# A hybrid decoder layer on one core: the prologue in the order the first product needs, three weight tiles in three passes each, and two weight pieces exchanged at the border of two products

## What is computed

```python
h = rmsnorm(x, norm_mix_g);  p = h @ w_in           # w_in: 2048 x 5120
o1, o2, o3, o4 = A_WIDTH, 2 * A_WIDTH, 2 * A_WIDTH + B_WIDTH, 2 * A_WIDTH + 2 * B_WIDTH
u = jax.nn.gelu(p[..., :o1]);  v = rmsnorm(jax.nn.gelu(p[..., o1:o2]), sgu_norm_g)
bg, cg, xb = p[..., o2:o3], p[..., o3:o4], p[..., o4:]
y_a = u * chunk_sgu(v, w_s, b_s)
zc, new_mix = causal_dwconv(cg * xb, mix_prev, conv_mix_w, conv_mix_b)
y = concatenate([group_rmsnorm(y_a, ...), group_rmsnorm(bg * zc, ...)], axis=-1)
x = x + y @ w_out
h = rmsnorm(x, norm_ffn_g)
gate, new_ffn = causal_dwconv(h @ w_gate, ffn_prev, conv_ffn_w, conv_ffn_b)
x = x + (jax.nn.silu(gate) * (h @ w_up)) @ w_down   # then a final rmsnorm
```

## Time and profile before

| what | value |
|---|---|
| median of three runs | 2260.38 us (2256.43, 2260.38, 2260.46) |
| the profiled execution | 2259.35 us, of which the span is 2257.7 us |
| PE busy | 2213.3 us, 98% of the span |
| DVE, ACT, POOL busy | 78%, 49%, 24% |
| mean granted clock of TensorE | 0.994 |

### The profile page before, as it was taken

One profiled execution on the slowest core, in us unless ns is written; L12 is line 12 of the kernel. 1 busy time (PEld: TensorE's weight loads), 2 busy tenths in 40 slices (PEclk: granted clock), 3 DMA queues, 4 the chain that ended last, 5 costly groups with the idle time before them and its releaser, 6 DMA issues. The chain is left out here.

```text
span 2257.7 us, 43328 instructions
## 1 busy us (share of the span) xinstructions
PE 2213.3 (98%) x16612; PEld 2199.4 (97%) x16612; DVE 1757.0 (78%) x2354; ACT 1111.4 (49%) x1758; POOL 547.2 (24%) x685
## 2 busy tenths in 40 slices
PE   6999999999999999999999999999999999999997
PEld 6999999999999999999999999999999999999997
DVE  5677777878333998888888888888888798888886
ACT  6454543444211554544445445444544665555565
POOL 4001111212222111111111011111112365555573
PEclk8999999999999999999999999999999999999998
DMA  7444345557433334443535353444446667765433
GB/s 226 100 141 115 113 118 156 181 164 248 133 96 95 115 112 144 138 155 120 159 126 159 118 162 125 149 127 153 137 138 226 205 204 243 233 221 200 165 108 106
DMA packets 377575, 346.05 MB, mean 153 GB/s; under 512 B 10474, under 2 KB 350629, under 8 KB 372720
## 3 DMA queue, kind: packets, MB, share of 16 engines
q1 hardware_dynamic: 346608, 203.98, 31.1%
q0 software_dynamic: 30848, 140.46, 17.4%
HBM read 273.40 MB, written 71.00 MB: 153 GB/s over the span
## 5 line engine op out<-in xcount | busy, mean ns | idle before, releaser
L3017 PE MATMUL ps<-form,dw_hi 128*128 128x288 f32 x1204 | 357.5, 297 | 4.5 <-DVE dw_lo L2458 2.1
L3018 PE MATMUL ps<-form,dw_hi 128*128 128x288 f32 x1204 | 354.4, 294 | 0.0
L3019 PE MATMUL ps<-form,dw_lo 128*128 128x288 f32 x1204 | 353.9, 294 | 0.0
L2956 PE MATMUL ps<-hq,w_hi 128*128 128x288 f32 x1008 | 298.4, 296 | 1.8 <-DVE w_lo L2302 1.8
L2957 PE MATMUL ps<-hq,w_hi 128*128 128x288 f32 x1008 | 296.8, 294 | 0.0
L2958 PE MATMUL ps<-hq,w_lo 128*128 128x288 f32 x1008 | 296.3, 294 | 0.0
L2458 DVE TENSOR_TENSOR dw_lo<-down,dw_hi 128x512 fp32r<-128x512 f32 (+1 forms) x280 | 236.9, 852 | 72.9 <-ACT dw_hi L1101 72.1
L3017 PEld LDWEIGHTS ps<-form,dw_hi 128*128 128x128 f32 x1204 | 225.8, 188 | 6.1 <-issue 5.4
L3018 PEld LDWEIGHTS ps<-form,dw_hi 128*128 128x128 f32 x1204 | 227.6, 189 | 0.0
L3019 PEld LDWEIGHTS ps<-form,dw_lo 128*128 128x128 f32 x1204 | 227.3, 189 | 0.0
L1541 ACT ACTIVATE w_hi<-raw 128x1024 fp32r<-128x1024 f32 x168 | 176.8, 1052 | 74.8 <-DMA raw<-in_w_gate_dram 68.4
(11 more groups left out here) (409 smaller groups left out, 6536.4 us busy)
## 6 DMA issues: line engine op xcount, KB each, us to landing
raw<-in_w_gate_dram SPq DMA_DIRECT2D x88, 512.0 KB, 4.6
down<-in_w_down_dram SPq DMA_DIRECT2D x32, 1024.0 KB, 5.5
form<-act_scratch POOLq DMA_DIRECT2D x28, 1152.0 KB, 7.1
act_scratch<-stage POOLq DMA_DIRECT2D x45, 576.0 KB, 4.7
raw<-in_w_in_dram SPq DMA_DIRECT2D x44, 512.0 KB, 4.8
raw_c<-in_w_up_dram SPq DMA_DIRECT2D x42, 512.0 KB, 3.8
raw_d<-in_w_up_dram SPq DMA_DIRECT2D x42, 512.0 KB, 5.3
raw<-in_w_out_dram SPq DMA_DIRECT2D x30, 512.0 KB, 4.0
```

The lines of the kernel that those rows point to most:

```text
L2956: te.matmul(out, w_hi[:, c, j, :], b_form(t, 0, j), start=start and j == 0, stop=False, skip_group_check=True)
L3017: te.matmul(out, dw_hi[:, m % 4, j, :], act_f[:, j, 0, :], start=start and j == 0, stop=False, skip_group_check=True)
L3018: te.matmul(out, dw_hi[:, m % 4, j, :], act_f[:, j, 1, :], start=False, stop=False, skip_group_check=True)
L3019: last = te.matmul(out, dw_lo[:, m % 4, j, :], act_f[:, j, 0, :], start=False, stop=stop and j == n - 1, skip_group_check=True)
```

## The change

Seven things are different.

1. PE transposes x tiles 0, 1 and 2, then begins. Three weight tiles (0, 1, 2) are worked in the first half and again in the second, each in three passes of 16 matmuls (`pre_part`): high x high over all 16 blocks, then low weight x high h, then high weight x low h. The transposes of x tiles 3 and 4 stand between the second and the third pass of tiles 1 and 2 of the first half. Weight tile 3 follows by `gemm`.
2. Units take banks by a table (X_BANK), so that tile 1 need not wait for tile 0's banks; the pairs of product banks are PRE_PAIR.
3. ACT and DVE take the units by kind of work instead of unit by unit. ACT: three squares, stages 0 to 3, high parts 0 to 7, weight pieces 0 and 1, stage 4, high parts 8 to 11, and on. DVE: all twelve gains, low parts 0 to 7, low parts of weight pieces 0 and 1, low parts 8 to 11, and on.
4. Weight tile 1 (pieces 2 and 3) is loaded into raw_z, which lies over x_nat[1], once x tiles 0 and 1 are transposed; tile 2's high and low parts (w_hi2, w_lo2) lie over x_nat[0] and x_nat[1]. Its reload of `raw` starts as soon as pieces 0 and 1 are split.
5. The column form t4f, which lies in the same place as w_hi2, is now made by ACT after piece 6 is done, and with it DVE's two low forms and all behind them.
6. POOL issues the loads of ws_nat and bias_b ahead of the last four stage transfers instead of behind them.
7. At the border, `raw_y` is loaded with piece 1 and `raw[:,0]` with piece 3; ACT and DVE follow, SP waits one low part longer before its loop, and ACT makes the high parts of the last two blocks of y before the first two weight pieces of the loop instead of behind them.

```diff
-    SKIP = 5 * WVIS + 2
+    SKIP = 5 * WVIS + 4
-        PRE_SLOT = (0, 1, 2, 3, 1, 0, 2, 3)
+        PRE_SLOT = {0: 0, 1: 1, 2: 2, 3: 3, 6: 2, 7: 3}
+        PRE_PAIR = (0, 1, 2, 1)
+        w_hi2 = sb("w_hi2", [P, 2, PK, P], F32R, at=n_at)
+        w_lo2 = sb("w_lo2", [P, 2, PK, P], F32R, at=n_at + 8192)
+        raw_z = sb("raw_z", [P, 2, PK, P], at=n_at + 8192)
+        X_BANK = (4, 5, 6, 7, 0, 1, 2, 3, 4, 5, 6, 7, 1, 3, 6, 7, 5, 6, 7, 5)
...
@@ SP @@
-            for n in range(1, PRE):
-                tile2(w_in, HEADS + n, 2 * n)
+            sp.wait_ge(x_t, 8)
+            for s in range(2):
+                sp.dma_start(raw_z[:, s], col(w_in, HEADS + 1, s)).then_inc(rawz_landed[s], 16)
+            for n in range(2, PRE):
+                for s in range(2):
+                    sp.wait_ge(lo_ready, s + 1 if n == 2 else 2 * n - 1 + s)
+                    sp.dma_start(raw[:, s], col(w_in, HEADS + n, s)).then_inc(raw_landed[s], 16)
...
-            sp.dma_start(raw_y[:, :, :], col(w_out, 1, 1)).then_inc(rawy_landed, 16)
+            sp.dma_start(raw_y[:, :, :], col(w_out, 1, 0)).then_inc(rawy_landed, 16)
             sp.wait_ge(lo_ready, IN_PIECES - 2)
-            sp.dma_start(raw[:, 0], col(w_out, 1, 0)).then_inc(raw_landed[0], 16)
+            sp.dma_start(raw[:, 0], col(w_out, 1, 1)).then_inc(raw_landed[0], 16)
             sp.wait_ge(lo_ready, IN_PIECES)
             sp.dma_start(raw[:, 1], col(w_out, 0, 1)).then_inc(raw_landed[1], 16)
+            sp.wait_ge(lo_ready, IN_PIECES + 4)
...
@@ POOL @@
             for u in range(4 * (TB + 1)):
+                if u == 4 * TB:
+                    pool.wait_ge(x_t, 4 * TB)
+                    g.dma_start(ws_nat[:, :, :], w_s[0].rearrange("h i j -> i h j")).then_inc(late_landed, 16)
...
@@ ACT @@
-            x_square(0)
-            x_square(1)
-            for tb in range(TB + 1):
-                for kq in range(4):
-                    x_unit(4 * tb + kq)
-                    if (tb, kq) in ((0, 1), (2, 3), (3, 1)):
-                        x_square({0: 2, 2: 3, 3: 4}[tb])
...
+            for tb in range(3):
+                x_square(tb)
+            x_stage(range(0, 4))
+            x_hi(range(0, 8))
+            pre_hi(0, 0)
+            pre_hi(1, 0)
+            x_stage(range(4, 5))
+            x_hi(range(8, 12))
+            x_stage(range(5, 8))
+            pre_hi(2, 0)
+            x_square(3)
+            pre_hi(3, 0)
...
+            act.wait_ge(t_sub, 4)
+            act.wait_ge(piece_done, 6)
+            a.activation(t4f[:, 0, :, :], xq(slice(0, PJ), 1, 0), ACT.Copy).then_inc(t_hi, 1)
...
-            first_hi(1, raw[:, 0], (raw_landed[0], 16 * (PRE + WVIS + 1)), (sum_done, 4 * WVIS))
+            first_hi(1, raw_y[:, :, :], (rawy_landed, 16), (sum_done, 4 * WVIS))
...
@@ DVE @@
+            x_gain(range(0, 1))
+            x_diag(1)
+            x_gain(range(1, 6))
+            x_diag(2)
+            x_gain(range(6, 12))
+            for u in range(8):
+                x_lo(u)
+            pre_lo(0)
+            pre_lo(1)
+            for u in range(8, 12):
+                x_lo(u)
+            x_diag(3)
+            pre_lo(2)
+            pre_lo(3)
+            x_gain(range(12, 16))
...
-                    first_lo(1, raw[:, 0])
+                    first_lo(1, raw_y[:, :, :])
...
@@ PE @@
+            def pre_part(tile, half, part):
+                cols = slice(half * HALF, (half + 1) * HALF)
+                for kk in range(KT):
+                    s, k = kk // PK, kk % PK
+                    q = 2 * tile + s
+                    unit = (4 * TB if half else 8) + kk // 4
+                    if part == 0:
+                        if k == 0:
+                            pe.wait_ge(hi_ready, q + 1)
+                        if kk % 4 == 0:
+                            pe.wait_ge(xhi_ready, unit + 1)
+                    elif part == 1:
+                        if k == 0:
+                            pe.wait_ge(lo_ready, q + 1)
+                    elif kk % 4 == 0:
+                        pe.wait_ge(xlo_ready, unit + 1)
...
             for half in range(2):
+                for tile in range(3):
+                    pe.wait_ge(xT_copied, ((5, 7, 9), (13, 14, 20))[half][tile])
+                    pre_part(tile, half, 0)
+                    pre_part(tile, half, 1)
+                    if half == 0 and tile >= 1:
+                        x_transposes(tile + 2)
+                    pre_part(tile, half, 2)
...
+            pe.wait_ge(tile_read, 2)
+            gemm(6, (PRE_SLOT[6], PRE_SLOT[7]), PRE_PAIR[3], mid=corner)
```

More of the change, by code:

```diff
@@ L327, in build_layer @@
         rawx_landed = sem("rawx_landed")
+        rawz_landed = [sem(f"rawz_landed{i}") for i in range(2)]
         rawy_landed = sem("rawy_landed")
@@ L2661, in params_t @@
                 for h in range(HEADS):
-                    last = te.transpose(ps[:, 4 + h // 4, (h % 4) * P:(h % 4 + 1) * P], ws_nat[:, h, :], ident[:, :])
+                    last = te.transpose(ps[:, 6 + h // 4, (h % 4) * P:(h % 4 + 1) * P], ws_nat[:, h, :], ident[:, :])
                 last.then_inc(param_t, 1)
@@ L2691, in _ @@
-            for t in (2, 3):
-                pe.wait_ge(tile_read, t - 1)
-                gemm(2 * t, PRE_SLOT[2 * t:2 * t + 2], t % 2, mid=params_t if t == 2 else corner)
+            def pre_part(tile, half, part):
[14 more added lines that the diff above has]
+                        pe.wait_ge(xlo_ready, unit + 1)
+                    w = pre_lo_of(q) if part == 1 else pre_hi_of(q)
+                    x = h_lo if part == 2 else h_hi
+                    last = te.matmul(pair(PRE_PAIR[tile], half), w[:, k, :], x[:, kk, cols],
+                                     start=part == 0 and kk == 0, stop=part == 2 and kk == KT - 1)
+                    if part == 2 and half == 1 and k == PK - 1:
+                        last.then_inc(piece_done, 1)
```

195 lines of the change are left out of this document (96 added, 99 removed).

## The result

The changed kernel takes 2249.15 us (median of 12 runs, 2243.66 to 2254.81); the kernel before, on the same chip, 2262.66 (12 runs, 2256.43 to 2268.85). The ratio of the runs is 0.9941, 95% interval [0.9928, 0.9953]: faster by 0.6%, 13.3 us. The profiled executions stand 9.96 apart (2259.35 and 2249.39; spans 2257.7 and 2247.8), where the forecast was 11.2. The forecast median of 2249.2 was met by 0.05; how much of that is chance is said further down.

A forecast was written before the change was run, and what follows sets the result against it. PE, busy 98% of the span, bounds the kernel with its waits and slow clock, mostly in the first slice. Prologue 9.9 plus border 1.3 gave 11.2 us: profiled 2259.35 to 2248.2, median 2249.2, range 2244.8 to 2253.0.

The forecast's parts named there:

- The first hole: Prologue, after the 96 transpose rows: PE idles 2.5 us, 20.7 to 23.2, until ACT's high part 8 is done.
- The second hole: Prologue, after the first pass: PE idles 2.1 us, 25.4 to 27.5, until DVE's first weight low part is done.
- the first rival: The clock falls in the new prologue holes; free in the first, 1.5 to 3 us after the second: 2250.7 to 2252.2, chance 0.17.
- No further hole to tile 3's end: Prologue from the second pass to tile 3: PE has no idle time; x tile 3's transposes take 3.7 us.
- raw_z was cheap as forecast: Prologue load of weight tile 1: issued at about 17, takes 8 us, lands at 25; ACT wants it at 26.2.
- The clock after x tile 4: Matmuls behind x tile 4's short transposes: the clock falls as before, 1.3 us lost, bounds 0 and 1.3.
- a half clock of more than 7 us in the first 60: Sign of being wrong: a half clock standing for more than about 7 us of the first 60.
- The first visit: First visit: the later form t4f delays DVE's low parts; 1.1 us more lost, 1.5 in all, bounds 0.4 and 3.
- The border: Border: PE restarts 1.3 us earlier, idle falls to 0.6, y block 14's sum of squares late next; bounds 0 and 1.4.
- late stage transfers: Prologue: stage 4's transfer may come at 25.5, the first product 3 late; price 1 to 2, 2250.2 to 2251.2, chance 0.10.
- the clock staying down: From 27.5 on each matmul takes 0.24 instead of 0.135; at 60 us the kernel stands at about 2261; chance 0.02.
- "Better": No clock fall after x tile 4 (1.3) and no extra loss in the visit (1.1): 2246.8 us, chance 0.15.

The follow-up runs named there:

- the filled version: Changed kernel with x unit 8 transposed three times more behind x tile 2, where PE had nothing to do: 2245.79 us, ratio 0.9933.
- the prologue alone: Changed kernel with the border put back as before, leaving only the prologue's part of the change: 2249.43 us, ratio 0.9954.
- the five executions: Same instructions up to the visit: changed kernel twice, border put back, y block 14's squares first, split_hi order put back; visit's matmul at 103.57, 101.30, 99.65, 103.02, 99.68.
- the halves: Changed kernel with each of the four operations of forms t4f and Xr ahead of the first visit cut in two: 2245.13 us, ratio 0.9921.
- the mixed transposes: Changed kernel with x tile 4's 16 short transposes put one by one between the matmuls of weight tile 2's second pass: 2257.6 us, ratio 0.9985.
- the edits together: Changed kernel with x unit 8's extra transposes, forms in halves, x tile 4's transposes in four groups, y block 14's squares first: 2240.57 us, ratio 0.9909.

## Why the prediction was right, step by step

- **The number, and luck.** The median was met by 0.05, and this is chance. The forecast took 11.2 from a base of 2260.38, the median of three runs; the same kernel's median over 12 runs is 2262.66. The ratio gives 13.3. A gain put 2.1 too small and a base 2.3 too low cancel. The mechanism, an earlier product with shorter holes, is borne out by the rows below; the sizes were off in both directions.
- **The first hole.** Forecast: product at 23.2. Measured: 23.28, released by ACT's high part, and 23.3 to 23.8 in the other executions of this order. Right, by the chain that the forecast named, though its sum slipped: from the four stages at 16.3, its own durations (8 x 0.52, 2.01, 0.50, 0.52) end at 23.5. The stages were done at 15.96, which made up for it.
- **The second hole.** Forecast: the second pass from 27.5. Measured: 27.25 (27.02 to 27.28 in others). Right in time. In the changed kernel's profile it shows no idle time, because the first pass ran at half clock and ended just then, as the first rival had it; in the filled version it shows as 1.32.
- **No further hole to tile 3's end, its transposes in 3.7.** 3.73, none. Right. raw_z was cheap as forecast: landed by 26.0, wanted there.
- **The clock after x tile 4.** Forecast: 1.3 lost, as before. This is the term that was mis-sized for this profile: against an execution without a fall there (the prologue alone) the two passes took 6.95 and not 4.35, the transposes themselves 4.17 and not 3.71, and the fall in the first hole, held to cost nothing, put the third pass 0.86 back (30.31, 29.45). Together 3.92, which is the whole distance between the two (103.57 and 99.65). Over the five executions the matmul stands at 101.44 in the mean; the forecast put it at 112.00 - 9.9 = 102.1. So the mean is right within 0.7 and this profile is a slow case. The forecast had named a half clock of more than 7 us in the first 60 as the sign of being wrong; it was 13.6 here (6.8 and 6.8), so by its own sign the forecast failed on the clock. What saved the sum is that most of the first fall lay over a wait, and that two of the five executions had no fall at x tile 4, where the forecast took 1.3 lost.
- **The account.** The losses in the profile after are 2.87 + 1.87 + 3.92 + 1.45 = 10.1 against 17.3 before: 7.2, where the rows show 8.43. So 1.3 of loss before was overlooked. Some 0.2 is in the short transposes (3.97 instead of 3.78), and 0.7 is in those of x tiles 0 to 2: between the holes their 96 rows took 5.59, 2.17 and 3.91, that is 11.67, and 10.96 in one piece after. Each hole cost more than its idle time. The last 0.4 is not traced.
- **The first visit.** Forecast 1.5 at two products; measured 1.03 + 0.42 = 1.45. Right, and the halves show the cause of the 1.03.
- **The border.** Forecast: PE restarts 1.3 earlier with 0.6 idle, and the sum of squares is late next. Measured: 9.54 - 8.23 = 1.31, 0.62, and 1.32 given back at that sum. What the forecast had wrong is the clock: it said that what the clock gives is behind that same sum. In fact the sum took the 1.31 and the clock gave 1.56 (9.78 - 8.22). And the exchanged order on ACT, costed at nothing, keeps a wait of 1.41 to 1.79 out by the rows; what it is worth in the mean is not well shown. Nor was it seen that PE's earlier arrival has a price: before 517.2 it waited 2.57 to 3.28 for the sum's low part, later 0.67 to 1.52.
- **The rivals.** The clock in the holes did happen; late stage transfers were 0.9 us away; the clock staying down did not happen with this order, but the mixed transposes show that it can (13.6 us). "Better" was the nearest of them to the truth: the ratio's 13.3 is a gain above the forecast's 11.2.

## What to carry to other kernels

A hole of PE can have two prices, its length and what the granted clock takes behind it; the second is not a constant of the program but varies from execution to execution, so read it over several runs (span x (1 - clock)) and not from one profile, and look where it lies, since over a wait it costs nothing. Compare a version with the kernel before on the same chip: that kernel alone differed by 3.5 +-1.1 between two of the chips, more than most of the single edits are worth. Ahead of an engine's queue ask what stands there that nobody wants yet: at the border and in the visit the order, or halves of a long operation, took the wait out of the rows. That this shortens the kernel is shown for the edits together, not for each. An edit costed at nothing should be costed again with PE arriving earlier, since that is what the rest of the change does.

## What was not expected of the hardware

- One instruction stream gives different clock patterns. After a first hole of 2.85 to 3.33 us the clock was at half for 6.8 us in two of nine profiles, for 3.4 in six and not at all in one; at x tile 4's transposes, where they stand in a row, for 6.8 us in one of ten, 3.4 in six, and not at all in three. Where PE was kept busy through the hole, no fall was seen there in the two profiles. The Trainium skill, page TensorE: Matmul & The Clock Gate, section Part 1: The HAM clock gate (the "warmup" mystery), says of the slow stretch at a kernel's start that it differs from run to run, because the chip's watching of the engine is not started with the kernel. These executions show such differences for later falls (99.65 to 103.57 for one matmul); their reason no run here shows.
- Sixteen narrow transposes mixed one by one with matmuls held the clock at half for 13.6 us, twice as long as the same ones in a row ever did, and cost 0.69 a pair at full clock instead of 0.37; in groups of four between passes they brought no fall in any of the three profiles that had them so, at a price of 1.0 for the groups.
- Twelve needless transposes in an idle stretch went with a kernel 4.0 +-1.0 us faster (5 and 6 runs), though only 0.05 of it can be found in the prologue of the two profiles.
